# The second block's context half leads and the latent half follows: output products, first and last MLP tiles, gated k and v once for each half

## The reference

```python
for i in range(2):
    m_lat = split((silu(c) @ w_mod[i] + b_mod[i]), 6)          # modulation rows
    m_ctx = split((silu(c_ctx) @ w_mod[i] + b_mod[i]), 6)
    h_lat = rms_norm(x_lat, g_pre_mix[i]) * (1 + m_lat[1]) + m_lat[0]
    h_ctx = rms_norm(x_ctx, g_pre_mix[i]) * (1 + m_ctx[1]) + m_ctx[0]
    y_lat, y_ctx = mixer(h_lat, h_ctx)     # i = 0: windowed GQA with sink; i = 1: gated linear attention
    x_lat = x_lat + m_lat[2] * rms_norm(y_lat, g_post_mix[i])
    f_lat = square(relu(modulate(x_lat) @ w_mlp_in[i])) @ w_mlp_out[i]    # hidden width 4096
    x_lat = x_lat + m_lat[5] * rms_norm(f_lat, g_post_mlp[i])
    # for i = 0 alone the same two updates are made for x_ctx
return x_lat
```

## Time and profile before

| | us |
|---|---|
| median of 3 runs | 2593.82 (2588.68 to 2593.93) |
| profiled execution, its own time | 2591.83 |
| its span in the trace | 2590.5 |
| PE busy | 2434.4 |
| DVE, ACT, POOL busy | 1217.1, 959.7, 501.5 |

### The profile page before, as it was taken

How to read it: one execution, slowest core, us unless ns; L and a number is a source line. 1 busy time by engine, 2 the same in 40 slices (tenths; PEclk the granted TensorE clock), 3 DMA queues, 4 the chain that set the end, 5 groups by cost and what they waited for, 6 DMA issues and landing times. The chain is left out here.

```text
span 2590.5 us, 37994 instructions
## 1 busy us (share of the span) xinstructions
PE 2434.4 (94%) x16773; PEld 2192.3 (85%) x16773; DVE 1217.1 (47%) x1560; ACT 959.7 (37%) x1125; POOL 501.5 (19%) x465
## 2 busy tenths in 40 slices
PE   7999899999999998889999899989999999888998
PEld 6999899979999996569998776888888888658998
DVE  5655556546555553446545344252123253454443
ACT  4433444334434433334443343233222223533442
POOL 2212333302212211212121100012112220230221
PEclk9999999999999998889999897779999989877998
DMA  7554433345555555775554100112222222202551
GB/s 243 169 178 163 133 128 115 114 164 180 188 170 190 183 173 194 252 257 179 184 178 136 49 17 17 33 66 98 97 95 94 93 89 98 98 0 81 180 180 65
DMA packets 203054, 344.60 MB, mean 133 GB/s; under 512 B 8829, under 2 KB 65258, under 8 KB 202890
## 3 DMA queue, kind: packets, MB, share of 16 engines
q1 hardware_dynamic: 202890, 342.18, 40.0%
HBM read 341.11 MB, written 1.05 MB: 132 GB/s over the span
## 5 line engine op out<-in xcount | busy, mean ns | idle before, releaser
L444 DVE TENSOR_TENSOR WL<-raw,WH 128x2048 fp32r<-128x2048 f32 (+2 forms) x281 | 651.5, 2330 | 699.8 <-ACT WH L431 699.8
L458 PE MATMUL PS<-XH,WH 128*128 128x256 f32 (+1 forms) x2336 | 702.1, 301 | 23.5 <-DVE WL L444 14.9
L458 PE MATMUL PS<-XL,WH 128*128 128x256 f32 (+1 forms) x2336 | 696.3, 298 | 0.0
L458 PE MATMUL PS<-XH,WL 128*128 128x256 f32 (+1 forms) x2336 | 696.0, 298 | 0.0
L431 ACT ACTIVATE WH<-raw 128x2048 fp32r<-128x2048 f32 (+2 forms) x281 | 518.7, 1858 | 367.0 <-PE PS L458 366.5
L458 PEld LDWEIGHTS PS<-XH,WH 128*128 128x128 f32 x2336 | 455.8, 195 | 37.1 <-DVE WL L444 16.0
L458 PEld LDWEIGHTS PS<-XL,WH 128*128 128x128 f32 x2336 | 456.2, 195 | 10.1
L458 PEld LDWEIGHTS PS<-XH,WL 128*128 128x128 f32 x2336 | 455.5, 195 | 10.2
L458 PE MATMUL PS<-al,al 128*128 128x64 f32 (+7 forms) x1376 | 298.2, 366 | 13.0 <-DVE al L2823 9.3
L458 PE MATMUL PS<-WH,XH 128*128 128x256 f32 (+2 forms) x912 | 277.5, 304 | 11.7 <-DVE XL L615 7.7
L458 PE MATMUL PS<-HH,WH 128*128 128x256 f32 x960 | 272.0, 283 | 1.6 <-DVE WL L444 1.6
(11 more groups left out here) (226 smaller groups left out, 2613.8 us busy)
## 6 DMA issues: line engine op xcount, KB each, us to landing
raw<-in_ffn_w_in SPq DMA_DIRECT2D x88, 1024.0 KB, 5.2
raw<-in_w_mod SPq DMA_DIRECT2D x48, 1024.0 KB, 5.3
raw<-in_ffn_w_out SPq DMA_DIRECT2D x40, 1024.0 KB, 5.0
raw<-in_a_w_in SPq DMA_DIRECT2D x36, 1024.0 KB, 5.0
raw<-in_w_mlp_in SPq DMA_DIRECT2D x32, 1024.0 KB, 5.5
raw<-in_w_mlp_out SPq DMA_DIRECT2D x32, 1024.0 KB, 5.0
raw<-in_gla_w_in SPq DMA_DIRECT2D x12, 1024.0 KB, 5.2
raw<-in_attn_w_qkv SPq DMA_DIRECT2D x6, 1024.0 KB, 4.9
```

Of the source, the lines that this page charges most:

```text
L444: dve.e.tensor_tensor(self.WL[j % NRAW][:, 0:nk * nn], self.raw[j % NRAW][:, 0:nk * nn], wh.bitcast(F32), ALU.subtract).then_inc(*self.lo. ...
L458: return self.pe.e.matmul(out, l, r, start=start, stop=stop, skip_group_check=skip)
```

## The change

The order of the halves is turned round, and each half gets its own pass over the weights.

- `last_products_*`, `pe_halves*`, `rest_*` and `gated_pool` go. `pe_part` makes 512 output features for one half with 256 columns, in 8 steps of 12 products, and yields after each.
- Attention: in g = 3 the context's result is transposed in iterations 10 and 11, and from iteration 12 on two such steps of its output product follow each iteration (`lead_pe`). Then come the rest of it, the transposes of the latent half, and its output product with the context's norms between its steps (`follow_pe`, `norms_pe`).
- The first two MLP tiles become four parts: context tile 0 and 1, latent tile 0 and 1, with the latent norms between their steps (`MLP_FIRST`, `mlp_first_act`).
- The last MLP group's output product: all of the context (lead), then all of the latent half (follow). The gated linear attention: k and v of the context, then q, k, gate and v of the latent half.
- The modulation fillings move into iteration 12 of g = 0, 1, 2 of the attention.
- The squares for the second norm go to the place of XL (`squares`), and the normed values to Y's place (`y_place`).

```diff
+    def pe_part(self, src, half, xs, banks, name, tag=""):
+        pe = self.pe
+        for i in range(2):
+            c, wh, wl = self.pe_chunk(src[512 * i:512 * i + 512, 512 * half:512 * half + 512], 4, 512, tag)
+            for b in range(4):
+                bank, at, o = banks[b // 2], 256 * (b % 2), slice(b * 128, b * 128 + 128)
+                for k in range(4):
...
+                    self.mm(out, wh[:, k, o], xh, kt == 0 and b % 2 == 0, False, True)
+                    self.mm(out, wh[:, k, o], xl, False, False, True)
+                    m = self.mm(out, wl[:, k, o], xh, False, kt == 7, True)
...
+                yield
+    def lead_pe(self, t, src, xs, first):
+        for half, banks in enumerate(self.LEAD[t][0]):
+            for _ in self.pe_part(src, half, xs, banks, (t, "o", half, 0)):
+                yield
+            self.empties(banks, self.y_made(first, (t, half, 0)))
+    def follow_pe(self, t, src, xs, first):
+        norms = self.norms_pe(t, 0)
+        for half, banks in enumerate(self.LEAD[t][1]):
+            for _ in self.pe_part(src, half, xs, banks, (t, "o", half, 1)):
+                next(norms, None)
...
+    def norms_pe(self, t, h):
...
+        yield
+        self.pe_sums(y, h, 0, YSQ, self.sq, (t, 0, h), b, True)
+        yield
+        yield
+        self.pe_sums(y, h, 1, YSQ, self.sq_act, (t, 1, h), b, False)
+        self.empties([b, b + 1], (self.mean, y))
+        yield
+        yield
+        self.pe_spread(y, h, b)
+        self.empties([b], (self.rstd_, y))
+        for _ in range(7):
             yield
...
         for q in range(2):
+            self.pe_sums(n, h, q, SQ, self.sq_act, (n, q), b2, False)
+        self.empties([b2, b2 + 1], (self.mean, n))
+        yield
+        yield
+        self.pe_spread(n, h, b2)
...
+    def norms_dve(self, t, h, first, l, sub, between):
...
+        self.dve_mean(y, h, self.PS[:, b:b + 2, 0], (y, 1))
+        self.dve_spread(y, h, b)
         for q in range(2):
+            self.gated_dve(t, h, q, l, sub, y, self.y_made(first, (t, q, h)))
+        self.dve_begin()
+        between()
+        self.dve_mean(n, h, self.PS[:, b2:b2 + 2, 0], (n, 1))
+        self.dve_spread(n, h, b2)
+        self.dve_begin()
+        self.prenorm_dve(n, h, *self.next_norm(l, sub), self.y_place(t, h), [])
...
-            H = self.hidden(T, lambda kt: ("mlp", l, grp, kt // nb))
+            H = self.hidden(T, lambda kt: ("mlp", l, grp, 3 if l == grp == 0 else kt // nb))
...
+    def mlp_first_act(self):
...
+        self.act_begin(2)
+        self.squares_act("gridn1", 1, self.tiles(self.squares[1]), [[(self.res, ("grid", 1, q))] for q in range(2)])
+        for v, banks in enumerate(self.MLP_FIRST):
+            key = ("mlp", 0, 0, v)
+            sg, hf = self.sg(v % 2, 4), self.hf(v % 2, 4)
+            act.wait_ge(self.lin, ("mlp", 0, 0, "in", v))
...
+            act.e.activation(four(sg), self.part(banks), ACT.Relu).then_inc(*self.evac.up(key))
+            self.act_begin()
+            act.wait_ge(self.mul, key)
+            act.e.activation(self.first_hidden(self.mHH, v), four(hf), ACT.Copy).then_inc(*self.hh.up(key))
+            if v == 0:
+                self.prenorm_act("gridn1", 1, 0, 1, self.y_place("grid", 1))
+            if v < 3:
+                self.act_begin()
...
+                if g < 3 and i == 12:
+                    self.pe_mods.send((0, 1))
+                if g == 3 and i in (10, 11):
+                    self.turn_o_pe("go0", self.cO[:, 0:2, :], (self.o_done, ("grid", 3, 0)), 0, (0, 1, 0, 1), range(2 * i - 20, 2 * i - 18))
+                if g == 3 and i > 11:
+                    next(lead), next(lead)
...
+        for _ in lead:
+            pass
+        self.turn_o_pe("go1", self.cO[:, 2:4, :], (self.o_done, ("grid", 3, 1)), 1, (2, 3, 6, 7))
+        self.follow_pe("grid", w_o, self.x_of("go1", 1), True)
...
+        keys(0, (0, 1))
+        for n, banks in enumerate(((2, 3), (0, 1))):
+            by_tokens(1024 + 512 * n, banks, 0, ("gla", "v", n, 0))
+        for _ in self.pe_part(w[:, 0:512], 0, x[1], (2, 3), ("gla", "q"), "gla"):
+            pass
+        self.empties([2, 3], (self.evac, ("gla", "q")))
+        keys(1, (4, 5))
         pe.wait_ge(self.v_step, ("gla", "down"))
...
+        by_tokens(1024, (6, 7), 1, ("gla", "v", 0, 1))
+        gates(0)
+        by_tokens(1536, (2, 3), 1, ("gla", "v", 1, 1))
+        for n, banks in enumerate(((0, 1), (6, 7))):
+            by_tokens(2048 + 512 * n, banks, 1, ("gla", "g", n))
```

More of the change, by code:

```diff
@@ new lines, in lead_pe @@
+    def lead_pe(self, t, src, xs, first):
[8 more added lines that the diff above has]
+                next(norms, None)
+            self.empties(banks, self.y_made(first, (t, half, 1)))
+        for _ in norms:
+            pass
@@ L2016, in rest_pool, with lead_act, follow_act @@
[L2016 to L2018 removed]
+    def lead_act(self, t, half, first, free):
+        self.to_y_act((t, half, 0), half, 0, self.part(self.LEAD[t][0][half]), (t, "o", half, 0), first, True, free)
+    def follow_act(self, t, first, l, sub, free):
+        lat = lambda half: self.to_y_act((t, half, 1), half, 1, self.part(self.LEAD[t][1][half]), (t, "o", half, 1), first, True, free)
+        self.act_begin(2)
+        self.squares_act(f"{t}n0", 0, self.tiles(self.squares[0]), [[(self.res, (t, 0, q))] for q in range(2)])
+        lat(0)
+        self.act_begin()
+        self.prenorm_act(f"{t}n0", 0, *self.next_norm(l, sub), self.y_place(t, 0))
+        self.act_begin()
+        lat(1)
@@ new lines, in follow_dve, with lat, lead_pool @@
+    def follow_dve(self, t, first, l, sub, before):
+        def lat(half):
+            if not first:
+                self.to_y_dve((t, half, 1), half, 1, self.part(self.LEAD[t][1][half]), (t, "o", half, 1), before(half, 1))
+        self.dve_begin()
+        self.norms_dve(t, 0, first, l, sub, lambda: lat(0))
+        self.dve_begin()
+        lat(1)
+    def lead_pool(self, t):
+        self.y_fold_pool((t, 0, 0), 0)
+        self.pool_pow(f"{t}y0", 0)
+        self.pool_pow(f"{t}n0", 0)
+        self.y_fold_pool((t, 0, 1), 1)
@@ L2131, in mlp_act @@
                 if l == 0:
-                    self.last_products_act("mlp0", False, 0, 1, free)
+                    for half in range(2):
+                        self.act_begin(2)
+                        self.lead_act("mlp0", half, False, free)
+                    self.follow_act("mlp0", False, 0, 1, free)
                 else:
@@ L2155, in mlp_dve @@
                 if l == 0:
-                    self.last_products_dve("mlp0", False, 0, 1, before)
+                    for half in range(2):
+                        self.dve_begin(2)
+                        self.lead_dve("mlp0", half, before)
+                    self.follow_dve("mlp0", False, 0, 1, before)
                 else:
@@ L2307, in grid_pe @@
             pass
+        lead = self.lead_pe("grid", w_o, self.x_of("go0", 0), True)
         for g in range(4):
@@ L2388, in grid_act @@
             pass
+        turned = [(self.turned, ("grid", "q", 3, 1))]
         for g in range(4):
@@ L2466, in grid_dve @@
                     pv(g, i - 2)
-        for h in range(2):
-            self.turn_o_dve(f"go{h}", h)
-        self.last_products_dve("grid", True, 0, 0, None)
+                if g < 3 and i == 12:
+                    self.dve_mods.send(1)
+                if g == 3 and i in (10, 11):
+                    self.turn_o_dve("go0", 0, range(2 * i - 20, 2 * i - 18))
+                if g == 3 and i in (12, 14, 16):
+                    self.dve_begin()
+        self.dve_begin()
+        self.turn_o_dve("go1", 1)
+        self.follow_dve("grid", True, 0, 0, None)
     def grid_pool(self):
```

406 lines of the change are left out of this document (165 added, 241 removed).

## The result

The changed kernel takes 2605.22 us (median of 6; 2601.42 to 2610.66) against 2588.99 (median of 6) for the kernel before: ratio 1.0060, 95% interval 1.0042 to 1.0079. So it is slower, by 0.4 to 0.6%, where I had forecast 2593.5 us and no difference. The forecast's own case ended at 2600 us; the wider range to 2608 holds the measured time only because of rival B. The profiled execution took 2601.42 us, the fastest of the six.

The account below looks back on a forecast made before the run. PE, busy 2434.4 of 2590.5 us, bounds the kernel, so only its waits, needless work or half clock matter. Terms 7.2 - 12.8 + 3.4 + 1.9 - 0.1 = -0.4 us gave 2593.5 us; range 2577 to 2608.

Parts of the forecast that it names:

- forecast's own case: Whole kernel: all terms hold as summed, 2593.5 us, own range 2588 to 2600; chance 0.40.
- rival B: Follow and first tiles: DVE's weight splits late at pieces 7, 11 and 13, +12 us, 2606; chance 0.18.
- term 3: MLP groups 1 and 2: ACT's weight split, one piece ahead, stands between a tile's end and its Relu, +3.4 us.
- term 1: Attention groups 0 to 2, iteration 12: modulation fillings back to back on PE, nothing hides them, +7.2 us.
- 3, 5 the rest of GLA: GLA's end: ACT's split ahead of the square after the output product, +1.9 us; the filling taken out, 0.
- Term 2: Attention's iteration 12 to the end of the first MLP tiles: 163.1 us before, 150.3 after, so -12.8 us.
- Term 4: Last group's lead to GLA's gates, from 2047.8 to 2240.3: 192.5 us before, 192.4 after, so -0.1 us.
- A: Attention g = 3: mixing attention and products doesn't lift the clock, +20 us, 2614; chance 0.07.
- C: Attention g = 3: go0's transposes in iterations 10 and 11 lift the clock at once, -7 us, 2586.5; chance 0.17.
- D: Norms: hidden, the split fits ahead of the spread, restarts at full clock cost nothing, -18 us, 2575.5; chance 0.12.
- E: MLP and GLA: ACT is not ahead, so no extra splits, -7 us, 2586.5; chance 0.06.
- The slower outcome: Whole kernel measurably slower than before: the clock-low and DVE-late rivals plus 0.04 of the forecast's case; chance 0.29.

Follow-up runs that it names:

- e1: Changed kernel with one act_begin less in mlp_first_act, so ACT is never a weight split ahead from the last first tile on; 2596.0 us.
- e2: Changed kernel with group 0's products asking for hidden tile 2 for kt 0 to 3, tile 3 only for kt 4 to 7, in banks 6 and 7; 2598.27 us.
- e4: Changed kernel with the dve_begin ahead of prenorm_dve moved ahead of the mean, in all four uses of norms_dve; 2595.84 us.
- e8: Changed kernel with the lead of the attention's output product behind the last six attention steps, not between them; 2611.14 us.
- c_after: The changed kernel measured again, as it is, beside other kernels; ratio 1.0037 to the kernel before.
- e10: Changed kernel with ACT's order, hidden tiles, fillings and prenorm split edited, last lead reordered, GLA's sixth weight split ahead of the latent prenorm; 2565.72 us.
- e7: Kernel before with only the three modulation fillings moved, into iteration 12 of the attention's groups 0 to 2; 2592.3 us.
- e6: Changed kernel with two modulation fillings behind the follow, turns in the bank the spread has just left, last turn at GLA's end; 2596.13 us.

## Why the prediction was wrong

What failed are sizes, not the mechanisms: the prediction let gains of 12.9 us and costs of 12.5 us cancel, and every term came out dearer. Most of it is term 3, ACT's split ahead of the Relu, sized at 3.4 us and measured at 7.6; then term 1, the fillings in the attention, sized at 7.2 and measured at 10.2. By its own terms, in the profiled execution; the sums run to where MLP(1) starts:

```
term                                    predicted   measured   by
1 fillings in the attention                 +7.2      +10.2    offset 0 to 10.2
2 attention's tail to end of group 0       -12.8      -10.1    10.2 to 0.1
3 ACT ahead: groups 1 and 2                 +3.4       +7.6    0.1 to 7.7
4 last group's lead to GLA's gates          -0.1       +1.2    7.7 to 8.9
3, 5 the rest of GLA                        +1.9       +3.1    8.9 to 12.0
sum                                         -0.4      +12.0
```

**Term 3 failed most**, by 4.2 us. Its mechanism is right: `mlp_first_act` begins one piece too many and the split stands ahead of the Relu. The size isn't: I priced a wait of 1.7 us per group, with every other duration as before (by the prediction's own figures, 12.2 + 1.9 - 12.15, it should have been 1.95). The same shift puts DVE's split under POOL's multiplication (3.09 for 1.90 us). That makes 2.85 us per group, and taking it out gave back 7.6 us over the two groups (from 1785.68 in e1 to its lead, against the same in the changed kernel), so what the waits don't hold goes with them. Clock is part of it: 0.73 over the 6.3 us behind the wait at 1888.71, where e1 has 1.00. At GLA's end the wait for the square grew by 1.86 us, as priced. The whole stretch from the transposes of GLA's output to MLP(1) is 52.4 us (2342.78 to 2395.22) against 47.9 in e1; e2 and e4, which keep the extra split, have 51.8 and 51.7. So the split goes with more than its wait there; in the changed kernel some of the rest lies ahead of it (clock 0.83 over the first 10 us, 1.00 in e1), and I can't say how much it is to blame for.

**Term 1** was 3.0 us too small. "3.1 us of PE back to back" left out the moved step's other half: `fill_act` and the sending on DVE bring weight splits along, which stood ahead of the chain that PE waits for in the second filling. The first filling cost 3.2 us and the turn 0.9, as priced.

**Term 2** was right in its parts. Clock full within iteration 12 (0.55, then 1.00): right, and e8 prices it at 8 to 9.4 us (8.1 and 1 to 3 forecast). Restarts of 3.2 us idle: 2.91. HL of group 0: 6.7 forecast, 7.48 measured, as POOL's last subtraction took 3.18 us and not 2.40. Its tiles are strided, but so are those of the first subtraction, which took 2.38; the slow ones have a WL split of DVE beside them (last section). It is the same omission as in term 3. The 2.7 us missing in the sum are no more than one execution differs from the next: in `c_after` the same stretch is 3.0 us shorter.

**Term 4**: the two waits in the lead, 2.9 and 4.7 us forecast, are 3.99 and 3.65, in sum the same. Of the two waits for WL in GLA, 2.8 and 3.6 forecast, one of 2.71 us is there. That one belongs to the sixth piece, as e10 shows. The term is 1.3 us off in all.

**Rivals.** A (clock low): no, 1.00 from 1645. B (DVE late at places 7, 11, 13) has nearly the measured time, 2606, but not its mechanism: at the three places PE waits 0.2 us or less; the time is a coincidence. C (the transposes lift the clock): no, it is 0.50 until 1640, though go0's transposes stand at 1627.70 and 1634.05, and 0.55 in 1640 to 1645, in iteration 12. The Trainium skill ("TensorE: Matmul & The Clock Gate", Part 4: PE-mode transpose) says that they don't count as activity, and this trace, with 0.50 behind 16 of them, agrees; the kernel before, whose clock rose during 32 of them in a row, doesn't, and neither does e7 (0.50, then 0.72 in 1660 to 1665, while its 32 run from 1657.68 to 1663.9). D (norms hidden): no, e4 and e6 show what hiding them takes. E (ACT not ahead): no; e1 is E made true, and it was worth 9 us by the first median (5.6 by the second) for the 7 I gave it. The slower outcome had 0.29; only the 0.04 in it for the forecast's own case with dearer waits is what happened, A and B are not. What I lacked is a case in which several terms are off the same way, since the work that moves along with a step (a split, an overlap of DVE and POOL) was left out of all of them.

## What to carry to other kernels

Where a change moves one engine's order by a step, price what starts beside it as well, not only what stands behind it: here the second effect was 1.2 us on top of 1.8. A step moved between engines' loops brings its bookkeeping with it; count the splits that it triggers on ACT and DVE at the new place, and the bank that its result waits in. The overlap that was planned came as planned (8 to 9 us); it was lost at four places with a cause of a line or two each, and all four stood in the prediction's working: three as waits, one as "nothing hides it".

## What the runs showed that I had not expected

DVE and POOL slow each other, and the one that starts second pays. The same 128x1024 multiplication takes 3.09 us when it starts within a WL split of DVE and 1.90 with none, while that split takes 2.29, its usual time. The other way round it is the split that is long: the first two rows and the last two of the next fence, from the first MLP tiles of the changed kernel, overlap by 1.33 us each, and each time the later one takes 1.2 us more than alone.

```profile
1757.37 2.29 DVE L446 TENSOR_TENSOR WL<-raw,WH 128x2048 fp32r<-128x2048 f32 x1 [1.19 <-ACT WH L433]
1758.33 3.09 POOL L2183 TENSOR_TENSOR TMP<-TMP 128x1024 f32<-128x1024 f32 x1 [12.75 <-ACT TMP L2127]
1760.09 3.48 DVE L446 TENSOR_TENSOR WL<-raw,WH 128x2048 fp32r<-128x2048 f32 x1 [0.42 <-ACT WH L433]
```

```profile
1743.20 2.38 POOL L2189 TENSOR_TENSOR al<-TMP,al 128x1024 fp32r<-128x1024 f32 x1
...
1781.68 3.18 POOL L2189 TENSOR_TENSOR al<-TMP,al 128x1024 fp32r<-128x1024 f32 x1 [1.17 <-ACT al L2130]
```

The second fence has the subtraction of group 0 without and with a split beside it (DVE's from 1780.37 to 1782.66). The mean of the multiplication over groups 1 to 3 went from 2.49 to 1.89 us when ACT's order kept the two apart (e1).

Executions of one kernel differ ahead of anything changed. In `c_after` the row with the wait of 2.06 us, just ahead of group 2, stands 7.9 us later than in the first profile (1551.09 against 1543.23), having lost it in small steps, most of them between 1010 and 1160; from group 3 to MLP(1) it is then 3.0 us shorter. In the stretches that I compared the clock differs (1100 to 1120: 0.79 and 0.66; 1140 to 1160: 1.00 and 0.77); why it does is open. The six executions of the changed kernel lie at 2601.4 to 2602.6 (three) and at 2607.8 to 2610.7 (three), and its median of 2605.22 in the gap between them. One profile therefore tells a term only to about 3 us, and the median of five or six runs has let two measurements of one kernel differ by 3.6 us.

The clock also falls where PE never waits: around the row sums at 1700.14 to 1704.83 in the changed kernel (32 of one column, 4.69 us) the stretch has 0.75 and the next one 0.57, both fully busy, behind 1.00 up to 1700. In `c_after` the same 32 take 3.63 us from 1708.22, still at full clock, and the stretch from 1711 to 1716 has 0.66, fully busy too. No run takes the sums away, so that they are the cause is not shown.

```profile
1700.14 4.69 PE L460 MATMUL PS<-ONES,al 128*128 128x1 f32 x32
```

```profile
1700.00:1705.00 5.00, 5.00 (x36) 0.75 0.60 201
1705.00:1710.00 5.00, 5.00 (x27) 0.57 0.00 0
```
